# A running sum on VectorE for stick-breaking attention, and another order of its last units

## The chip, the cores and the metric

The kernel runs on one core of a Trainium2 chip. The metric is the device time of one execution in microseconds (us). TensorE (PE) multiplies matrices into PSUM, VectorE (DVE), ScalarE (ACT) and GpSimd (POOL) compute elementwise, SyncE (SP) issues the transfers. TensorE's clock is granted at one of two levels, 1.2 or 2.4 GHz; a profile gives the granted clock of a stretch as a share of the full one.

## The reference, cut to what matters

The program is two blocks of two layers each. The change is in the first block, whose layers mix four groups of heads, gate them and project them:

```python
def stick_breaking_attention(q, k, v):
    ...
    def step(args):
        qblk, i = args
        z = jnp.einsum('bqhd,bkhd->bhqk', qblk.astype(jnp.float32), kf) * scale
        qpos = i * BLOCK + jnp.arange(BLOCK)
        mask = kpos[None, :] < qpos[:, None]
        log_keep = jnp.where(mask, jax.nn.log_sigmoid(-z), 0.0)
        after = lax.cumsum(log_keep, axis=3, reverse=True) - log_keep
        a = jnp.where(mask, jnp.exp(jax.nn.log_sigmoid(z) + after), 0.0)
        return jnp.einsum('bhqk,bkhd->bqhd', a, vf)
...
    y = jnp.stack([ya, yb, yc, yd], axis=2)
    y = rmsnorm(y, g_grp.reshape(N_GROUPS, GROUP_WIDTH)).reshape(b, s, D_MIX)
    y = y * jax.nn.silu(gate)
    return x + rmsnorm(y @ w_out, g_post)
```

There are 512 positions, 4 heads of 64 in this group, and blocks of 128 keys. For each query the weight of a key needs the sum of log_keep over all later keys up to the query.

## The kernel before, in words

Everything is stored transposed, features on the partitions and the 512 positions along the free dimension, in chunks of 128 features. Matrix products with weights use fp32 split in a high and a low part (fp32r): ScalarE writes the high part of a weight slot of 128x1024 (`w_high`), GpSimd and VectorE the two halves of its low part (`w_low`), and TensorE makes three products of it, 8 matmuls each. Slots stream through a ring of four. The same is done to activations: `y_high(c)` (ScalarE, L1426) writes XH, `y_low` (VectorE for odd chunks, GpSimd for even ones, L2337) writes XL.

The order of work on each engine is written out by hand; semaphores connect them. Stick-breaking attention is cut into eight units: two pairs of heads (hp 0 and 1), and in each the key blocks k = 3, 2, 1, 0, the last first. Unit u has scores for queries from block k on, of width 512-128k for each of the two heads, in two PSUM banks (`z_banks`). Its steps are:

- `z_scores(u)`, TensorE L743 and L745: scores of both heads and the mask. From unit 2 on it waits for the exponential of unit u-2, which frees the banks.
- ScalarE L1437 to L1439: Abs, Exp and Ln into `prob_t`; then VectorE L1906 writes softplus(z) into `sp_ts`, which keeps the four blocks of the pair of heads.
- `keep_sums(u)`, TensorE L764: the scores once more, and onto them the negated sums: the block of k itself through a triangular matrix (`ntri`), each later block k2 through an all-ones matrix (`nones`), as plain fp32 matmuls. For k=0 these are four matmuls for each head, 512, 384, 256 and 128 wide.
- ScalarE L1450: the exponential of that is the weight `a_t`. After four units `stick_values(hp)`, TensorE L775, multiplies the values, and VectorE copies them (`stick_copy`, L1895).

Between the units stand pieces of other work. TensorE's loop (L830 to L848) runs for u = 1 to 8: a half product of the input projection while there are any (up to u = 5), `high_pair` of the output projection (L820, L821: y's high halves with the first two output slots, 28 and 29; two chunks at u = 7, two at u = 8), `z_scores(u)`, sums for group norms (L555), `keep_sums(u-1)`. `high_pair` at u = 7 waits for y's high halves, for the accumulators 28 and 29 (that is, for VectorE's `take` of gate chunk 7, L1753) and for both parts of the second slot. ScalarE's loop (L1428) runs the functions of unit u, the exponential of unit u-1, and the rest: slots, squares, `gate_sigmoids` (which load the sigmoid's table and load the old one back, L1418 and L1419), `y_high`. VectorE's loop (L1898) takes the last gate chunks before units 2, 4 and 6, makes low halves of slots, writes the softplus, computes a row of the second block's modulation (`modulation`, L1730, whose rows SyncE loads one by one in line with the weight slots), norms and gates.

## Time and profile before

| | us |
|---|---|
| median of the runs | 2401.52 |
| lowest and highest of 3 | 2398.0, 2401.79 |
| the profiled execution | 2396.37 |
| its span in the profile | 2394.6 |
| TensorE busy | 2254.8 (94%) |
| VectorE busy | 1655.5 (69%) |
| ScalarE busy | 1016.3 (42%) |
| mean granted clock of TensorE | 0.989 |

The span runs from the first to the last instruction; the execution's own time is 1.8 us longer. The stick-breaking units of layer 0 lie from about 221 to 307 us of the span, those of layer 1 from about 584 to 659 us for the part from the second unit on. Then each layer's output projection follows, and after layer 1 the second block, which the change does not touch. In the timelines a matmul's start is exact and its end modelled; the pitch from one start to the next is the time that it takes.

### The profile page before, as it was taken

The page shows a single profiled execution, that of the slowest core. Times are in us where ns is not written, and L with a number is a line of the kernel's source. Part 1 is how long each engine was busy: PE and PEld are TensorE (multiplying, and loading weights), DVE is VectorE, ACT ScalarE, POOL GpSimd, SP SyncE. Part 2 cuts the span into 40 slices and gives each one's busy share as a digit, 9 for nine tenths or more (in the row PEclk, how much of TensorE's full clock was granted, in tenths as well). Part 3 has the DMA queues.
Part 4 walks back from the last instruction along what each step waited for, and adds up shares of the span by engine and source line. Part 5 has one row for each costly group of instructions (what it writes and reads, how often), then busy time and mean ns, then how long its engine had stood idle before and what let it go on. Part 6 is the DMA issues. An engine that isn't in the chain of part 4 may idle for free.

```text
span 2394.6 us, 34614 instructions
## 1 busy us (share of the span) xinstructions
PE 2254.8 (94%) x11722; PEld 1774.6 (74%) x11722; DVE 1655.5 (69%) x2744; ACT 1016.3 (42%) x1665; POOL 695.2 (29%) x418
## 2 busy tenths in 40 slices
PE   8999899999788799989999999999999999999998
PEld 5766566766467689976767788888768677888886
DVE  8776578775588767545688576666566875766765
ACT  4344624344534456534254444442242634444421
POOL 3211143211142256642101333334321013333342
PEclk9999999999999999989999999999999999999999
DMA  6421234422143145543210244446531102434463
GB/s 216 168 80 54 88 106 146 158 71 71 62 158 118 52 141 184 177 143 121 78 36 1 97 141 146 144 144 225 180 133 53 37 18 88 156 134 155 140 233 140
DMA packets 81102, 286.88 MB, mean 120 GB/s; under 512 B 9009, under 2 KB 11218, under 8 KB 80564
## 3 DMA queue, kind: packets, MB, share of 16 engines
q1 hardware_dynamic: 80948, 284.95, 34.9%
q8 instruction: 81, 1.33, 0.2%
q14 instruction: 73, 0.60, 0.1%
HBM read 282.82 MB, written 2.10 MB: 119 GB/s over the span
## 4 chain that ended last, share of the span: by engine, by line
PE 49%; DVE 3%; issue 1%; ACT 1%; DVEq 0%; ACTq 0%
PE banks L1198 6%; PE banks L1204 6%; PE banks L1202 6%; PE banks L1220 3%; PE banks L1221 3%; PE banks L1227 3%; PE banks L887 3%; PE banks L888 3%; PE banks L892 3%; PE banks L1046 2%; PE banks L1065 2%; PE banks L1076 2%; PE banks L909 1%; PE banks L916 0%; DVE y_t L2216 0%
## 5 line engine op out<-in xcount | busy, mean ns | idle before, releaser
L1527 ACT ACTIVATE wh_t<-ring 128x1024 fp32r<-128x1024 f32 x264 | 279.1, 1058 | 496.6 <-PE banks L1204 297.9
L2007 DVE TENSOR_TENSOR wl_t<-ring,wh_t 128x512 fp32r<-128x512 f32 x264 | 203.3, 771 | 284.6 <-ACT wh_t L1527 279.6
L2364 POOL TENSOR_TENSOR wl_t<-ring,wh_t 128x512 fp32r<-128x512 f32 x132 | 223.1, 1693 | 470.8 <-ACT wh_t L1527 449.3
L2396 POOL TENSOR_TENSOR wl_t<-ring,wh_t 128x512 fp32r<-128x512 f32 x132 | 236.2, 1790 | 420.2 <-ACT wh_t L1527 420.1
L2331 POOL TENSOR_TENSOR wl_t<-ring,wh_t 128x512 fp32r<-128x512 f32 x72 | 126.0, 1753 | 450.6 <-ACT wh_t L1285 433.9
L1198 PE MATMUL banks<-xh_t,wh_t 128*128 128x512 f32 (+1 forms) x960 | 203.0, 354 | 0.0
L1202 PE MATMUL banks<-xh_t,wl_t 128*128 128x512 f32 (+1 forms) x960 | 203.0, 354 | 0.0
L1204 PE MATMUL banks<-xl_t,wh_t 128*128 128x512 f32 (+1 forms) x960 | 203.0, 354 | 0.0
L1220 PE MATMUL banks<-gh_t,wh_t 128*128 128x512 f32 (+1 forms) x528 | 180.5, 354 | 1.0 <-ACT wh_t L1527 1.0
L1221 PE MATMUL banks<-gl_t,wh_t 128*128 128x512 f32 (+1 forms) x528 | 180.3, 354 | 0.0
L1202 PEld LDWEIGHTS banks<-xh_t,wl_t 128*128 128x128 f32 x960 | 161.4, 189 | 25.0
L1198 PEld LDWEIGHTS banks<-xh_t,wh_t 128*128 128x128 f32 x960 | 161.4, 189 | 25.0
L1204 PEld LDWEIGHTS banks<-xl_t,wh_t 128*128 128x128 f32 x960 | 161.4, 189 | 24.9
L887 PE MATMUL banks<-xh_t,wh_t 128*128 128x512 f32 (+1 forms) x480 | 173.6, 374 | 4.1 <-ACT wh_t L1527 4.1
L888 PE MATMUL banks<-xl_t,wh_t 128*128 128x512 f32 (+1 forms) x480 | 164.0, 354 | 0.0
L1730 DVE CUSTOM_DVE_ANT_0 banks<-m_t 128x1024 f32<-128x1024 f32 x96 | 159.0, 1656 | 2.6 <-DMA m_t<-wmod_d 0.9
L2259 DVE CUSTOM_DVE_ANT_0 m_t<-m_t 128x1024 f32<-128x1024 f32 x96 | 153.1, 1595 | 5.7 <-DMA m_t<-wmod_d 4.5
L564 PE MATMUL banks<-xh_t,wh_t 128*128 128x512 f32 x320 | 127.8, 399 | 5.9 <-DVE y_t L1945 5.0
L565 PE MATMUL banks<-xl_t,wh_t 128*128 128x512 f32 x320 | 124.6, 390 | 0.0
L1227 PE MATMUL banks<-gh_t,wl_t 128*128 128x512 f32 (+1 forms) x528 | 114.6, 354 | 0.2 <-POOL wl_t L2364 0.2
L1220 PEld LDWEIGHTS banks<-gh_t,wh_t 128*128 128x128 f32 x528 | 99.8, 189 | 15.1 <-ACT wh_t L1527 1.2
L1221 PEld LDWEIGHTS banks<-gl_t,wh_t 128*128 128x128 f32 x528 | 99.8, 189 | 13.7
(394 smaller groups left out, 4562.5 us busy)
## 6 DMA issues: line engine op xcount, KB each, us to landing
ring<-w_d SPq DMA_DIRECT2D x338, 512.0 KB, 3.7
m_t<-wmod_d SPq DMA_DIRECT2D x160, 512.0 KB, 3.5
qh_t<-tables_d SPq DMA_DIRECT2D x6, 512.0 KB, 4.7
m_t<-tables_d SPq DMA_DIRECT2D x6, 512.0 KB, 5.4
par<-p_d SPq DMA_DIRECT2D x4, 696.0 KB, 6.4
x_t<-x_in_d SPq DMA_DIRECT2D x4, 512.0 KB, 6.6
big<-tables_d SPq DMA_DIRECT2D x2, 1024.0 KB
out_d<-x_t SPq DMA_DIRECT2D x4, 512.0 KB, 2.8
```

Source lines behind the costliest of these rows:

```text
L887: pe.matmul(dst, hi[:, k * P:(k + 1) * P], xh[k], start=k == 0, stop=False)
L888: pe.matmul(dst, hi[:, k * P:(k + 1) * P], xl[k], start=False, stop=False)
L1198: pe.matmul(dst, hi[:, k * P:(k + 1) * P], xh[k], start=k == 0, stop=False)
L1202: pe.matmul(dst, lo[:, k * P:(k + 1) * P], xh[k], start=False, stop=False)
L1204: mm = pe.matmul(dst, hi[:, k * P:(k + 1) * P], xl[k], start=False, stop=k == KD - 1)
L1220: pe.matmul(dst, hi[:, o:o + P], v["GH"][k + u], start=k + u == 0, stop=False)
L1221: pe.matmul(dst, hi[:, o:o + P], v["GL"][k + u], start=False, stop=False)
L1227: mm = pe.matmul(dst, lo[:, o:o + P], v["GH"][k + u], start=False, stop=k + u == FK - 1)
L1527: nc.scalar.activation(WH[j % 2], slot2(j), ACT.Copy).then_inc(sm2["w2_hi"], 1)
L2007: nc.vector.tensor_tensor(WL[j % 2][:, 512:1024], slot2(j)[:, 512:1024], WH[j % 2][:, 512:1024].bitcast(F32), ALU.subtract).then_inc(sm2[" ...
L2364: pool.tensor_tensor(WL[j % 2][:, 0:512], slot2(j)[:, 0:512], WH[j % 2][:, 0:512].bitcast(F32), ALU.subtract).then_inc(sm2["w2_lo_a"], 1)
L2396: pool.tensor_tensor(WL[q % 2][:, 0:512], slot2(24 + q)[:, 0:512], WH[q % 2][:, 0:512].bitcast(F32), ALU.subtract).then_inc(sm2["w2_lo_a"], 1)
```

## The change

Three things change.

1. VectorE adds up later blocks. When the softplus of a unit with k = 1 or 0 is written, VectorE waits until `keep_sums` of the unit before is through (`wz_ready`), and adds block k+2 onto block k+1 of `sp_ts` (all but its first 128 columns, which k+2 doesn't reach). `keep_sums` then needs one matmul through `nones` for each head, of block k+1, in place of one for each later block. It waits for the new semaphore `sp_summed`. 12 matmuls a layer go, four VectorE instructions come.
2. TensorE issues `z_scores(u)` directly behind the half product, so at u = 7 before `high_pair`.
3. ScalarE's last three gate sigmoids move from the end of step 5 into step 7, behind that unit's functions; the four high halves of y that stood in steps 6 and 7 all stand in step 6. VectorE's take of gate chunk 7 and the low half of slot 29 move behind the softplus of unit 6.

```diff
--- before.py
+++ after.py
@@ -85,7 +85,7 @@
     acc_ready=36, acc0_free=18, acc1_free=18, lat_up=8, kr_ready=1, lat_squared=3, lat_summed=2, lat_ready=3,
     qc_in=4, kvc_in=4, swap_ready=5, rot_ready=5, kr_copied=4,
     vt_ready=6, vt_copied=6, sc_ready=32, negmax=32, p_exp=32, p_norm=32, pt_ready=32, pt_copied=32,
-    o_ready=16, o_copied=16, z_ready=8, z_ln=8, sp_done=8, wz_ready=8, a_exp=8,
+    o_ready=16, o_copied=16, z_ready=8, z_ln=8, sp_done=8, sp_summed=4, wz_ready=8, a_exp=8,
     sbo_ready=2, sbo_copied=2, conv_done=2, y_squared=8, y_summed=4, y_normed=8,
     gate_sig=8, gate_mul=8, y_ready=8, z_squared=KD, z_added=KD - 2, z_summed=1, zn_ready=KD // 2, x_updated_a=4, x_updated_b=4,
     link_act=32, link_dve=LINK_DVE1,
@@ -757,12 +757,15 @@
 
                     hp, k = U[u]
                     pe.wait_ge(*at("sp_done", u + 1))
+                    if k < NT - 2:
+                        pe.wait_ge(*at("sp_summed", 2 * hp + NT - 2 - k))
                     masked_scores(u, False)
+                    last = min(k + 1, NT - 1)
                     for e, bank in enumerate(z_banks(u)):
-                        for k2 in range(k, NT):
+                        for k2 in range(k, last + 1):
                             o = e * 1280 + OFF[k2]
                             mm = pe.matmul(bank[:, (k2 - k) * P:T - k * P], ntri if k2 == k else nones, sp_ts[hp][:, o:o + T - k2 * P],
-                                           start=False, stop=k2 == NT - 1)
+                                           start=False, stop=k2 == last)
                     mm.then_inc(sm["wz_ready"], 1)
 
                 def stick_values(hp):
@@ -830,6 +833,8 @@
                 for u in range(1, len(U) + 1):
                     if pieces:
                         piece()
+                    if u < len(U):
+                        z_scores(u)
                     if u == 7:
                         acc_begin(28)
                         acc_begin(29)
@@ -839,8 +844,6 @@
                         high_pair(range(2))
                     elif u == 8:
                         high_pair(range(2, 4))
-                    if u < len(U):
-                        z_scores(u)
                     if u in (2, 3, 4):
                         group_sum(u - 2)
                     if u == 5:
@@ -1442,6 +1445,8 @@
                         w_high(26)
                     if u >= 1:
                         hp, k = U[u - 1]
+                        if u == 7:
+                            gate_sigmoids(range(5, KD))
                         act.wait_ge(*at("wz_ready", u))
                         if u == 1:
                             act.wait_ge(*at("conv_done", 2))
@@ -1456,14 +1461,10 @@
                         group_rstd(u - 2)
                     if u == 2:
                         gate_sigmoids(range(5))
-                    elif u == 5:
-                        gate_sigmoids(range(5, KD))
                     elif u == 6:
-                        y_high(0)
-                        y_high(1)
+                        for c in range(4):
+                            y_high(c)
                     elif u == 7:
-                        y_high(2)
-                        y_high(3)
                         group_square(3, (0,))
 
                 y_high(4)
@@ -1896,7 +1897,7 @@
 
                 U = units()
                 for u in range(len(U)):
-                    if u in (2, 4, 6):
+                    if u in (2, 4):
                         j = 24 + u // 2
                         take(j, H[GATE + j - 20])
                         w_low(j + 2)
@@ -1905,10 +1906,16 @@
                     dve.wait_ge(*at("z_ln", u + 1))
                     nc.vector.scalar_tensor_tensor(both(sp_ts[hp], k), z_both(u, w), 0.0, lz_both(u, w),
                                                    ALU.max, ALU.add).then_inc(sm["sp_done"], 1)
+                    if k < NT - 2:
+                        dve.wait_ge(*at("wz_ready", u))
+                        later = both(sp_ts[hp], k + 1)[:, :, P:]
+                        nc.vector.tensor_tensor(later, later, both(sp_ts[hp], k + 2), ALU.add).then_inc(sm["sp_summed"], 1)
                     if u == 0:
                         outs(TN // 2 - 1)
                         w_low(26)
                     elif u == 6:
+                        take(27, H[GATE + 7])
+                        w_low(29)
                         stick_copy(0)
                     modulation(16 + u)
                     if u in (3, 4, 5):
```

ScalarE (ACT), steps 5 to 7 of the loop, before; L1285 is a slot's high part, L1437 to L1439 the functions of a unit, L1450 an exponential, L1418 and L1419 the gate sigmoids with their tables, L1426 high halves of y:

```order
L1450 ACTIVATE big<-banks 128x2x128
L1285 ACTIVATE wh_t<-ring 128x1024
L1418 ACT_TABLE_LOAD
L1418 ACTIVATE vm_t<-big 128x512
L1418 ACTIVATE kh_t<-big 128x512 x2
L1419 ACT_TABLE_LOAD
L1437 ACTIVATE prob_t<-banks 128x2x384
L1438 ACTIVATE prob_t<-prob_t 128x2x384
L1439 ACTIVATE prob_t<-prob_t,eps_t 128x2x384
L1450 ACTIVATE big<-banks 128x2x256
L1426 ACTIVATE xh_t<-y_t 128x512 x2
L1437 ACTIVATE prob_t<-banks 128x1024
```

and now (L1440 to L1442 are the functions, L1455 the exponential, L1421 and L1422 the sigmoids, L1429 the high halves):

```order
L1288 ACTIVATE wh_t<-ring 128x1024
L1440 ACTIVATE prob_t<-banks 128x2x384
L1441 ACTIVATE prob_t<-prob_t 128x2x384
L1442 ACTIVATE prob_t<-prob_t,eps_t 128x2x384
L1455 ACTIVATE big<-banks 128x2x256
L1429 ACTIVATE xh_t<-y_t 128x512 x4
L1440 ACTIVATE prob_t<-banks 128x1024
L1441 ACTIVATE prob_t<-prob_t 128x1024
L1442 ACTIVATE prob_t<-prob_t,eps_t 128x1024
L1421 ACT_TABLE_LOAD
L1421 ACTIVATE vm_t<-big 128x512
L1421 ACTIVATE kh_t<-big 128x512 x2
```

The two table loads and three sigmoids moved from ahead of unit 6's functions to behind unit 7's, and the four high halves stand together ahead of unit 7's functions.

VectorE (DVE) around unit 6, before; L1879 and L1885 are a gate's products, L1753 the take of gate chunk 7, L1720 the low half of slot 29, L1906 the softplus, L1895 the copy of the first pair of heads, L1730 a modulation row:

```order
L1879 TENSOR_TENSOR big<-big,va_t 128x512
L1885 TENSOR_TENSOR y_t<-y_t,big 128x512
L1753 COPY big<-banks 128x512
L1720 TENSOR_TENSOR wl_t<-ring,wh_t 128x512
L1906 SCALAR_TENSOR_TENSOR big<-banks,prob_t 128x2x384
L1895 COPY y_t<-banks 128x512
L1730 ISA big,mtmp<-m_t 128x1024
```

and now (L1880, L1886, L1754, L1721, L1907, L1896 and L1731 are those; L1912 is the new sum):

```order
L1880 TENSOR_TENSOR big<-big,va_t 128x512
L1886 TENSOR_TENSOR y_t<-y_t,big 128x512
L1907 SCALAR_TENSOR_TENSOR big<-banks,prob_t 128x2x384
L1912 TENSOR_TENSOR big<-big 128x2x128
L1754 COPY big<-banks 128x512
L1721 TENSOR_TENSOR wl_t<-ring,wh_t 128x512
L1896 COPY y_t<-banks 128x512
L1731 ISA big,mtmp<-m_t 128x1024
```

The softplus and a sum of 2x128 stand ahead of the take and the slot's low half. The other three sums follow the softplus of units 2, 3 and 7 in the same way.

TensorE (PE) from unit 5's accumulation on, before; L743 and L745 are scores and mask, L764 the accumulation, L547 and L837 waits, L820 and L821 the output products (each of the last two rows comes four times in turn and stands here once):

```order
L764 MATMUL banks<-big,cst 128x128
L547 REGISTER_ALU
L837 REGISTER_ALU
L820 MATMUL banks<-xh_t,wh_t 128x512
L821 MATMUL banks<-xh_t,wl_t 128x512
L743 MATMUL banks<-big 128x512 x2
L745 MATMUL banks<-mask_r,ident_r 128x128 x2
L743 MATMUL banks<-big 128x384 x2
L745 MATMUL banks<-mask_r,ident_r 128x128 x2
L764 MATMUL banks<-big,cst 128x384
L764 MATMUL banks<-big,cst 128x256
L764 MATMUL banks<-big,cst 128x128
```

and now (L767 is the accumulation, L842 a wait, L823 and L824 the output products, the rows that only repeat left out in the same way):

```order
L767 MATMUL banks<-big,cst 128x128
L743 MATMUL banks<-big 128x512 x2
L745 MATMUL banks<-mask_r,ident_r 128x128 x2
L547 REGISTER_ALU
L842 REGISTER_ALU
L823 MATMUL banks<-xh_t,wh_t 128x512
L824 MATMUL banks<-xh_t,wl_t 128x512
L743 MATMUL banks<-big 128x384 x2
L745 MATMUL banks<-mask_r,ident_r 128x128 x2
L767 MATMUL banks<-big,cst 128x384
L767 MATMUL banks<-big,cst 128x256
```

Unit 7's scores, 512 wide, moved ahead of the output products, and unit 6's accumulation has lost the matmul 128 wide of each head.

## Rows read from the trace of the kernel before

**Rows 1.** Page, part 1: busy us (share of the span) and instructions of each engine

```profile
PE 2254.8 (94%) x11722; PEld 1774.6 (74%) x11722; DVE 1655.5 (69%) x2744; ACT 1016.3 (42%) x1665; POOL 695.2 (29%) x418
```

**Rows 2.** Waits of TensorE over the span: us in total, times, longest us

```profile
PE banks L820 <- ACT xh_t L1426: 21.2, 6, 7.6
...
PE banks L564 <- DVE y_t L1945: 5.0, 4, 2.0
```

**Rows 3.** Timeline of TensorE, layer 0: start us, us, engine, line, operation [idle before]

```profile
258.80 1.98 PE L555 MATMUL banks<-mw,cst 128*128 128x512 f32 x4 [1.48 <-ACT rstd_t L1277]
...
262.05 4.53 PE L764 MATMUL banks<-sp_even,cst 128*128 128x512 f32 x16
266.33 1.18 PE L681 MATMUL banks<-xl_t,wh_t 128*128 128x512 f32 x4
...
274.41 0.92 PE L743 MATMUL banks<-big 64*128 64x384 f32 x4 [0.47 <-ACT big L1450]
...
276.54 1.52 PE L764 MATMUL banks<-big,cst 128*128 128x256 f32 x8
285.69 0.76 PE L820 MATMUL banks<-xh_t,wh_t 128*128 128x512 f32 x1 [7.63 <-ACT xh_t L1426]
...
289.03 1.13 PE L743 MATMUL banks<-big 64*128 64x512 f32 x4
...
290.46 0.92 PE L743 MATMUL banks<-big 64*128 64x384 f32 x4
...
291.58 2.81 PE L764 MATMUL banks<-big,cst 128*128 128x384 f32 x12
295.81 0.51 PE L820 MATMUL banks<-xh_t,wh_t 128*128 128x512 f32 x1 [1.42 <-ACT xh_t L1426]
...
299.20 4.53 PE L764 MATMUL banks<-big,cst 128*128 128x512 f32 x16
304.93 2.38 PE L775 MATMUL banks<-big,vd_t 128*64 128x512 f32 x16 [1.19 <-ACT big L1450]
```

**Rows 4.** Busy us by stretch: PE, PEld, DVE, ACT, POOL, then PEclk, DMA share, GB/s

```profile
285.70:289.00 3.30, 3.30 (x8) 2.39 (x8) 3.27 (x5) 0.36 (x1) 1.19 (x1) 0.56 0.05 11
...
320.40:355.70 35.30, 34.83 (x148) 27.73 (x149) 34.56 (x41) 7.92 (x11) 21.31 (x12) 1.00 0.51 179
```

**Rows 5.** Timeline of ScalarE (ACT), layer 0, around the gate sigmoids

```profile
275.32 1.28 ACT L1418 ACT_TABLE_LOAD   x1
...
279.95 0.63 ACT L1418 ACTIVATE kh_t<-big 128x512 f32<-128x512 f32 x1 [2.19 <-DVE big L1753]
...
281.89 0.81 ACT L1437 ACTIVATE prob_t<-banks 128x768 f32<-128x768 f32 x1
...
284.45 0.58 ACT L1450 ACTIVATE big<-banks 128x512 f32<-128x512 f32 x1
284.93 1.14 ACT L1426 ACTIVATE xh_t<-y_t 128x512 fp32r<-128x512 f32 x2
290.57 1.02 ACT L1437 ACTIVATE prob_t<-banks 128x1024 f32<-128x1024 f32 x1 [4.50 <-PE banks L745]
```

**Rows 6.** Timeline of VectorE (DVE), layer 0

```profile
255.52 1.23 DVE L1906 SCALAR_TENSOR_TENSOR sp_even<-banks,prob_t 128x1024 f32<-128x1024 f32 x1 [10.88 <-ACT prob_t L1439]
...
275.50 1.76 DVE L1879 TENSOR_TENSOR big<-big 128x512 f32<-128x512 f32 x1
...
279.23 0.68 DVE L1753 COPY big<-banks 128x512 f32<-128x512 f32 x1
279.83 0.68 DVE L1720 TENSOR_TENSOR wl_t<-ring,wh_t 128x512 fp32r<-128x512 f32 x1
284.57 0.96 DVE L1906 SCALAR_TENSOR_TENSOR big<-banks,prob_t 128x768 f32<-128x768 f32 x1 [4.06 <-ACT prob_t L1439]
...
293.89 1.23 DVE L1906 SCALAR_TENSOR_TENSOR big<-banks,prob_t 128x1024 f32<-128x1024 f32 x1 [4.58 <-ACT prob_t L1439]
```

**Rows 7.** Timeline of GpSimd (POOL), layer 0

```profile
275.38 1.33 POOL L2331 TENSOR_TENSOR wl_t<-ring,wh_t 128x512 fp32r<-128x512 f32 x1 [16.38 <-ACT wh_t L1285]
```

## The prediction

> **What bounds the kernel now.** I read the page's busy shares first: TensorE is busy 94% of the span [rows 1], so only work taken off TensorE, or a wait in front of it, can pay. The list of waits then shows where it idles: its longest wait in total is L820, the first output products, for ScalarE's high halves of y (L1426), 21.2 us in six waits, the longest 7.6 [rows 2]. Each layer runs the stretch once, so a layer has half of that. TensorE's timeline of layer 0 shows the place [rows 3]: the cumulative matmuls (L764) of unit 5 start at 276.54, and after them TensorE stands still 7.63 us until 285.69; another 1.42 us end at 295.81. I read the rest of the argument from the stretch 262 to 305 of layer 0; layer 1 has the same waits (21.2 is twice 10.6) and is taken as equal.
>
> Why it waits is in ScalarE's timeline [rows 5]: at 275.32 it loads another function table, computes three sigmoids (the last held 2.19 us by VectorE's take of gate chunk 7), loads the old table back, and only at 281.89 begins unit 6; y's first two high halves come at 284.93. The granted clock was 0.56 in the 3.3 us behind the wait, so TensorE had fallen from 2.4 to 1.2 GHz while it stood still, and the eight products there took 3.34 us (285.69 to 289.03) [rows 3, 4].
>
> **The change, part by part.** All times in layer 0.
>
> *Fewer matmuls.* L764 of a unit with k=0 took 4.28 us (262.05 to 266.33) for 5120 record columns (4 records for each width: two heads, two records per fp32 matmul), 0.836 ns each [rows 3]. The change keeps widths 512 and 384: 3584 columns, 3.00 us, so 1.28 less. A unit with k=1 keeps 384 and 256 of 384, 256, 128: 0.43 less. Units with k=2 and 3 keep everything. That is 1.71 for each pair of heads, 6.8 us over two pairs and two layers. Of it the 0.43 of unit 2 is worth nothing: behind it TensorE waits 1.48 us for ScalarE anyway (258.80), and the wait grows by 0.43 [rows 3]. Unit 3's 1.28 is on the path, and everything behind it starts 1.28 earlier.
>
> *The running sum.* Four more VectorE instructions a layer, 2x128 wide for k=1 and 2x256 for k=0. No row shows this operation. The nearest is VectorE's subtraction of two SBUF operands 512 wide: 0.68 alone, 1.76 when GpSimd was in such a subtraction (its own began at 275.38 and took 1.33) [rows 6, 7]. So 0.3 to 1.76 for one; less than nothing is excluded, it is added work. I take 0.7 for k=0 and, where GpSimd works beside it, 0.9. Each sum also waits until the unit before has been accumulated, since that read the block unsummed; queued behind it stand the modulation row, gates, and so SyncE's next modulation load. Nothing is charged for units 2 and 3: before unit 3's softplus at 255.52 VectorE stood idle for 10.88 us, which takes up what unit 2's sum adds, and TensorE comes to unit 3's accumulation at 262.05, some 5 us after a sum that follows that softplus [rows 3, 6]. Unit 7: the previous accumulation ends at 286.9 (below), the sum is ready about 288.0, and TensorE is in the second pair of output chunks until 288.9: hidden by 0.9, with 1.76 it is just not.
>
> *The new order.* In my reckoning, TensorE ends unit 5's accumulation at 276.54+1.28-1.28 = 276.54. Unit 6's scores began at 274.41, now 273.1, ready about 274.4 [rows 3]. ScalarE is free at 275.32-1.28 = 274.0 because the sigmoids are gone from here; unit 6's three functions take 2.56 (281.89 to 284.45) and end at 277.0, its exponential of unit 5 at 277.6 [rows 5]. TensorE waits for that, 1.1 us, then runs unit 7's scores, which now come first: 1.43 (289.03 to 290.46), until 279.1 [rows 3]. ScalarE makes four high halves in a row, 0.57 each, from 277.6 to 279.8 [rows 5].
>
> Now VectorE is late next. Gate 3's product ended at 279.23, now 278.0 [rows 6]. Then come unit 6's softplus 0.96, the sum 0.9, the take of chunk 7 at 0.6 (279.23 to 279.83; it frees the accumulator that the output products need) and the low half of slot 29, between 0.68 and 1.76, taken at 1.2, since GpSimd is making low halves of y at that time. That is 281.65, when the output products start instead of 285.69: a wait of 2.55. The waits 7.63 and 1.42 are replaced by 1.1 and 2.55.
>
> The rest at full clock: first output pair 2.0 (3.39 from 295.81 to 299.20, less the 1.4 of scores in it), scores 1.12 (290.46 to 291.58), accumulation 2.56-0.43 = 2.13, ending at 286.9 [rows 3]. Unit 7's functions: ScalarE from 279.8, 3.3 us (290.57 to VectorE's start at 293.89), then the two tables and three sigmoids, which took 6.57 (275.32 to 281.89) less the 2.19 of wait, 4.4; all done at 287.5, then unit 6's exponential [rows 5, 6]. No one waits for that one. Second output pair with scores 3.39, without a wait as its halves are long made: 290.3. Accumulation 3.00: 293.3. Wait for the last exponential as before, 304.93-299.20-4.28 = 1.45 [rows 3]: the value matmuls L775 start at 294.75 instead of 304.93. **10.2 us a layer, 20.4 in both.** From L775 on the order is the same on every engine, and the 35.3 us behind it (320.40 to 355.70) have TensorE busy 34.83 of it [rows 4], so the gain passes on.
>
> The profiled execution took 2396.37 us, which gives 2376.0. The median of the runs shown stands 5.15 above it, at 2401.52, and 20.4 off that gives 2381.1. I predict 2381.
>
> **A rule weighed.** VectorE's gate product that began at 275.50 ended 0.55 us after GpSimd's 1.33 us were over [rows 6, 7]. The Trainium skill, page "SBUF — State Buffer", section "Who interferes with whom", says that a VectorE instruction with two SBUF inputs and a GpSimd one that reads SBUF exclude each other for their whole length, whoever starts first. By that rule the sum waits for GpSimd's first low half and slot 29's subtraction for its second: output products at about 281.6 and 20.4 us in all; if they ran undisturbed, 280.6 and 22.5 us. The trace agrees with the rule, and it speaks against a sum placed where four high halves set GpSimd to work.
>
> **Bounds of the forecast.** Undisturbed, VectorE is done at 280.6: 11.2 a layer, 2379. If both two-operand instructions take 1.76, it is 283.0: 8.9 a layer. If the clock also falls in the waits of 1.1 and 2.55 (one of 2.0 at L564 left it at 1.00 [rows 2, 4], the long one didn't), 1.4 a layer is lost (3.34 against 2.0 for a pair): 7.5 a layer, 2386.5. The runs shown spread 3.8 us.
>
> **Rivals.**
> 1. *The sum is on the path.* If unit 6's and unit 7's sums and their two hand-overs each hold TensorE for one contended subtraction, 1.76, a layer gains 10.2-3.5 = 6.7: 2388. For it: unit 7 has 0.9 us to spare. Against: units 2 and 3 have far more, and ScalarE's sigmoids are off this path.
> 2. *The long wait only changes its owner.* The output products need chunk 7's take and slot 29, both now behind the softplus of unit 6; if that is reached as late as the present 284.57 [rows 6], the products start near 287 and only the trimmed matmuls and the second wait remain: about 3.4 a layer at most, 2395. Against: 284.57 is caused by the sigmoids, which are gone.
> 3. *The stretch behind is fed too slowly.* It starts 10 us earlier, and in it the transfers use 0.51 of the DMA engines, at 179 GB/s [rows 4]. If two slots are late by 2 us each in each layer: 2389. Against: those slots are asked for by events that move along.
> 4. *The change does not save what it says*, as when the compiled order kept the sigmoids in front of the halves; the order shows that it doesn't. Nothing moves: 2401.
> 5. *Slower.* After the two waits TensorE stays at 1.2 GHz. From 281.65 to 294.75 it has 11.7 us of work, which would take 23.4; that alone costs 11.7 a layer against a gain of 10.2. The mechanism decides from 10.2 us of work at the low clock a layer on; at the full 11.7, it is 3 us slower, 2404.5, and more where it lasts into the output projection. For it: TensorE now idles twice within 5 us with only 1.43 of work between. Against: behind a wait of 7.63 the low clock lasted about 3.3 us.
>
> **How the numbers follow.** Forecast 0.76 (2379 to 2386.5), rival 1 0.09, rival 3 0.05, rival 2 0.04, rival 4 0.03, slower 0.03. A measurement of this kernel can tell about 0.2%, 4.8 us, from no change. Faster by more than that: the forecast and rivals 1 and 3 wholly, and 2 nearly, 0.94; same 0.03 (rival 4); slower 0.03. The range goes from 2375 (the upper bound of the gain, less the spread of the runs) to 2388.5 (rival 1 included).
>
> **What would show it.** L767 of a k=0 unit at 3.0 us; the wait before L823 near 2.5 instead of 7.6, ended by VectorE's slot subtraction and no longer by the high halves; granted clock 1.00 throughout 276 to 290; L778's second group near 294.7; no wait that VectorE's sum ends. Wrong: a wait of TensorE on the sum over 1 us, a clock of 0.6 after 281, or new DMA waits in the output projection.

## The result, and the profile after

| | before | after |
|---|---|---|
| median, us | 2399.76 (4 runs, 2396.89 to 2401.79) | 2381.72 (4 runs, 2380.27 to 2384.13) |
| the profiled execution, its span | 2396.37, 2394.6 | 2380.27, 2378.4 |
| TensorE busy | 2254.8 | 2249.5 |
| mean granted clock of TensorE | 0.989 | 0.989 |

The change is faster: the ratio is 0.9925, with a 95% interval of 0.9911 to 0.9939, so 18.0 us by the medians and between 14.6 and 21.4. The forecast was a gain of 20.4 and a time of 2381. The time was met within a microsecond, but part of that is luck: the gain inside the two stretches that the change touches was 15.1 us in the profiled pair, and two clock falls in each layer, which the sum had left out, make the difference. Laid from profile to profile, the forecast was 2376.0 and the measured time 2380.27.

The page of the changed kernel, part 1, as [rows 1]:

```profile
PE 2249.5 (95%) x11674; PEld 1767.7 (74%) x11674; DVE 1656.3 (70%) x2752; ACT 1015.3 (43%) x1665; POOL 687.5 (29%) x418
```

48 records of TensorE are gone (12 fp32 matmuls a layer, two records each, in two layers), and 8 instructions of VectorE have come. TensorE's waits, as [rows 2]: us in total, times, longest.

```profile
PE banks L823 <- DVE wl_t L1721: 4.7, 2, 2.4
...
PE banks L555 <- ACT rstd_t L1280: 3.4, 2, 1.7
PE banks L823 <- ACT xh_t L1429: 3.1, 2, 1.6
PE banks L743 <- ACT big L1455: 3.0, 6, 0.9
```

The waits of 7.63 and 1.42 for the high halves of y are gone. In their place stand 2.4 for VectorE's low half of slot 29 and 0.9 for ScalarE ahead of unit 7's scores. (What is left of L823 for `xh_t` are two waits of 1.56 in the output projection; before has them too.) No wait is ended by VectorE's sum. TensorE's timeline of layer 0, to be read against [rows 3]:

```profile
259.87 3.52 PE L555 MATMUL banks<-mw,cst 128*128 128x512 f32 x4 [1.70 <-ACT rstd_t L1280]
263.32 1.13 PE L743 MATMUL banks<-big 64*128 64x512 f32 x4
...
264.65 3.22 PE L767 MATMUL banks<-sp_even,cst 128*128 128x512 f32 x8
267.42 1.38 PE L681 MATMUL banks<-xl_t,wh_t 128*128 128x512 f32 x4
268.64 2.00 PE L685 MATMUL banks<-xh_t,wl_t 128*128 128x512 f32 x8
...
280.21 1.13 PE L743 MATMUL banks<-big 64*128 64x512 f32 x4 [0.87 <-ACT big L1455]
...
284.09 0.76 PE L823 MATMUL banks<-xh_t,wh_t 128*128 128x512 f32 x1 [2.38 <-DVE wl_t L1721]
287.39 0.92 PE L743 MATMUL banks<-big 64*128 64x384 f32 x4
...
293.98 3.22 PE L767 MATMUL banks<-big,cst 128*128 128x512 f32 x8
298.39 2.37 PE L778 MATMUL banks<-big,vd_t 128*64 128x512 f32 x16 [1.19 <-ACT big L1455]
```

Two things are to be seen. The third group sum (L555) took 3.52 us instead of 1.98, behind a wait that had grown from 1.48 to 1.70. And the first pair of output products took 3.30 (284.09 to 287.39), where 2.0 had been reckoned. Both are the clock, in the same four matmuls and the same eight. Busy us by stretch, PEclk the third from the end:

```profile
259.90:263.30 3.40, 3.40 (x4) 1.14 (x4) 3.40 (x7) 1.78 (x4) 0.00 (x0) 0.54 0.38 134
...
284.10:287.40 3.30, 3.30 (x9) 2.35 (x9) 3.27 (x6) 3.24 (x5) 0.00 (x0) 0.58 0.57 184
```

The group sum of before had PEclk 1.00. In layer 1 of the change both fell too (the group sum took 3.68, the pair 3.44).

VectorE, as [rows 6]: the four sums (L1912), and what stands between unit 6's softplus and the output products.

```profile
245.05 0.43 DVE L1912 TENSOR_TENSOR sp_even<-sp_even 128x256 f32<-128x256 f32 x1 [0.49 <-PE banks L767]
...
257.74 0.68 DVE L1912 TENSOR_TENSOR sp_even<-sp_even 128x512 f32<-128x512 f32 x1
...
280.53 0.95 DVE L1907 SCALAR_TENSOR_TENSOR big<-banks,prob_t 128x768 f32<-128x768 f32 x1
281.40 0.92 DVE L1912 TENSOR_TENSOR big<-big 128x256 f32<-128x256 f32 x1
282.24 0.68 DVE L1754 COPY big<-banks 128x512 f32<-128x512 f32 x1
282.84 1.15 DVE L1721 TENSOR_TENSOR wl_t<-ring,wh_t 128x512 fp32r<-128x512 f32 x1
...
290.92 0.69 DVE L1912 TENSOR_TENSOR big<-big 128x512 f32<-128x512 f32 x1 [2.73 <-PE banks L767]
```

and GpSimd beside it, as [rows 7]:

```profile
280.76 2.68 POOL L2344 TENSOR_TENSOR xl_t<-y_t,xh_t 128x512 fp32r<-128x512 f32 x2 [2.75 <-ACT xh_t L1429]
```

The sum 256 wide took 0.43 alone and 0.92 while GpSimd made low halves of y; the slot's low half took 1.15 instead of 0.68. ScalarE, as [rows 5]: unit 7's functions, both table loads behind them, and then still 1.22 us of idle time before unit 6's exponential. The sigmoids are off the path.

```profile
282.14 1.01 ACT L1440 ACTIVATE prob_t<-banks 128x1024 f32<-128x1024 f32 x1
...
285.44 1.28 ACT L1421 ACT_TABLE_LOAD   x1
...
288.42 1.28 ACT L1422 ACT_TABLE_LOAD   x1
290.92 0.82 ACT L1455 ACTIVATE big<-banks 128x768 f32<-128x768 f32 x1 [1.22 <-PE banks L767]
```

**How the experiments are read.** The executions of one program spread by up to 14 us, much of it outside the changed code, so each run is also read by the *stretch*: from the start of the layer's first group sum (L555) to the start of the second value matmuls (L775 or L778), which holds all that the change moves on TensorE from unit 2 on. Before it is 65.28 us in layer 0 (239.65 to 304.93) and 65.48 in layer 1. The change has 57.67 and 57.97: 7.6 and 7.5 less. "Group sum" and "pair" below are the time from the first matmul of the third L555 group, or of the first output products, to the next scores: 1.91 and 2.0 at full clock. Where the low clock lasts longer than the group or the pair, the scores behind it are slow too, and the table does not show that part; it is named below where it matters.

| run | stretch, layers 0 and 1 | wait, group sum (0; 1) | wait, pair (0; 1) |
|---|---|---|---|
| before | 65.28, 65.48 | 1.48, 1.91; 1.48, 1.92 | 7.63, 3.34; 7.63, 3.56 |
| the change | 57.67, 57.97 | 1.70, 3.45; 1.70, 3.61 | 2.38, 3.30; 2.37, 3.44 |
| after_again | 59.16, 56.41 | 1.70, 3.40; 1.70, 1.92 | 2.38, 3.68; 2.38, 3.16 |
| sum_only | 63.00, 64.44 | 1.70, 1.92; 1.70, 3.01 | 7.63, 3.68; 7.63, 3.68 |
| order_only | 56.60, 58.23 | 1.48, 1.92; 1.48, 2.81 | 1.06, 2.02; 1.06, 2.01 |
| take_first | 55.12, 55.03 | 1.70, 3.33; 1.70, 3.56 | 0.97, 2.02; 0.97, 1.99 |
| scores_behind | 57.61, 58.21 | 1.70, 1.91; 1.70, 3.56 | 3.33, 3.68; 3.33, 2.87 |
| sigmoids_back | 62.09, 62.16 | 1.70, 3.55; 1.70, 3.34 | none, 2.84; none, 2.94 (7.02 ahead of the scores) |
| order_take | 56.47, 56.51 | 1.48, 1.91; 1.48, 1.92 | 0.97, 1.99; 0.97, 2.02 |
| order_take_again | 58.04, 56.45 | 1.48, 1.91; 1.48, 1.91 | 0.97, 3.36; 0.97, 1.99 |
| change_fill7 | 56.47, 54.89 | 1.70, 3.55; 1.70, 1.92 | 0.17, 2.00; 0.18, 2.02 |
| change_filled | 54.84, 54.86 | 0.35, 1.91; 0.35, 1.91 | 0.17, 2.00; 0.18, 2.02 |
| fill_wait | 53.38, 53.39 | 0.35, 1.91; 0.35, 1.91 | 0.97, 1.99; 0.97, 1.99 |
| fill_again | 54.86, 53.42 | 0.35, 1.92; 0.35, 1.91 | 0.97, 3.47; 0.96, 2.01 |

### The profile page after: what moved, and what is told of

Same layout as the page of the kernel before. It is cut to its first block, busy times and chain, and to the rows that moved or that the text cites. A ratio compares the mean times of both kernels' runs of the same rounds, so it can differ in the third digit from the quotient of the medians.

```text
span 2378.4 us, 34534 instructions
## 1 busy us (share of the span) xinstructions
PE 2249.5 (95%) x11674; PEld 1767.7 (74%) x11674; DVE 1656.3 (70%) x2752; ACT 1015.3 (43%) x1665; POOL 687.5 (29%) x418
## 3 DMA queue, kind: packets, MB, share of 16 engines
q8 instruction: 80, 1.31, 0.2%
## 4 chain that ended last, share of the span: by engine, by line
PE 50%; DVE 3%; issue 1%; ACT 1%; DVEq 0%; ACTq 0%
PE banks L1207 6%; PE banks L1205 6%; PE banks L1201 6%; PE banks L1224 3%; PE banks L1230 3%; PE banks L1223 3%; PE banks L890 3%; PE banks L891 3%; PE banks L895 3%; PE banks L1049 2%; PE banks L1079 2%; PE banks L1068 2%; PE banks L912 1%; PE banks L907 1%; PE banks L908 1%
## 5 line engine op out<-in xcount | busy, mean ns | idle before, releaser
L2014 DVE TENSOR_TENSOR wl_t<-ring,wh_t 128x512 fp32r<-128x512 f32 x264 | 203.2, 771 | 286.4 <-ACT wh_t L1528 281.8
L2371 POOL TENSOR_TENSOR wl_t<-ring,wh_t 128x512 fp32r<-128x512 f32 x132 | 223.0, 1692 | 466.5 <-ACT wh_t L1528 445.0
L2403 POOL TENSOR_TENSOR wl_t<-ring,wh_t 128x512 fp32r<-128x512 f32 x132 | 236.3, 1791 | 420.1 <-ACT wh_t L1528 420.0
L2338 POOL TENSOR_TENSOR wl_t<-ring,wh_t 128x512 fp32r<-128x512 f32 x72 | 119.0, 1655 | 459.9 <-ACT wh_t L1288 443.9
L1731 DVE CUSTOM_DVE_ANT_0 banks<-m_t 128x1024 f32<-128x1024 f32 x96 | 156.8, 1633 | 3.1 <-DMA m_t<-wmod_d 1.4
L564 PE MATMUL banks<-xh_t,wh_t 128*128 128x512 f32 x320 | 129.5, 405 | 5.0 <-DVE y_t L1952 4.1
L1721 DVE TENSOR_TENSOR wl_t<-ring,wh_t 128x512 fp32r<-128x512 f32 x72 | 62.6, 870 | 69.0 <-ACT wh_t L1288 67.8
```

Source lines behind the costliest of these rows:

```text
L2014: nc.vector.tensor_tensor(WL[j % 2][:, 512:1024], slot2(j)[:, 512:1024], WH[j % 2][:, 512:1024].bitcast(F32), ALU.subtract).then_inc(sm2[" ...
L2371: pool.tensor_tensor(WL[j % 2][:, 0:512], slot2(j)[:, 0:512], WH[j % 2][:, 0:512].bitcast(F32), ALU.subtract).then_inc(sm2["w2_lo_a"], 1)
L2403: pool.tensor_tensor(WL[q % 2][:, 0:512], slot2(24 + q)[:, 0:512], WH[q % 2][:, 0:512].bitcast(F32), ALU.subtract).then_inc(sm2["w2_lo_a"], 1)
```

## The experiments

### The change taken apart

**The change once more** (no edit).

> The changed kernel once more, beside the others on one chip. If the lower clock behind the wait of 1.7 us at L555 (the four sums took 3.5 us and not 2.0 there) is the change's own, it shows again in both layers; if it was chance, at most one layer shows it. Time against the kernel before: 16 to 20 us less.

Measured: 2382.81 us (2381.15 to 2386.15, 5 runs), ratio 0.993 (0.9917 to 0.9944). The change's time holds. In layer 1 the group sum kept its clock behind the same wait of 1.70, so that fall does not come every time. The pair fell in both layers; in layer 1 its first two matmuls were still quick (0.47 and 0.39) and the rest slow, 3.16 for the eight. In layer 0 the low clock lasted beyond the pair: the scores behind it took 1.58 for 0.85 from start to start, and the fall cost 2.8 us in all, 1.5 more than in the first profile.

**Only the running sum**, on the order of before.

```
+ (VectorE, behind the softplus of units with k < 2)
+     nc.vector.tensor_tensor(later, later, both(sp_ts[hp], k + 2), ALU.add)
- for k2 in range(k, NT):
+ for k2 in range(k, min(k + 1, NT - 1) + 1):
```

> The running sum and the fewer matmuls alone, the order of the kernel before. Theory 1 (my terms stand, the clock at L555 was chance): 1.28 of unit 3, 0.43 of unit 6 (hidden in the wait of 1.42, so nothing) and 1.28 of unit 7 a layer, 2.6 to 3.0 a layer, 5.1 to 6.0 us in all. Theory 2 (fewer matmuls in unit 2 make the wait in front of the sums L555 longer, 1.70 for 1.48, and the clock falls there): the same less 1.5 a layer, so only 2 to 3 us, and L555 at 3.5 us. The wait of 7.6 us in front of the first output product stays under both.

Measured: 2396.82 us (2392.53 to 2399.89, 11 runs), ratio 0.9986 (0.9977 to 0.9995), so some 3 us; the stretches are 2.3 and 1.0 shorter. With what the clock took counted back (in layer 0 0.8 more than in before, behind the wait of 7.63; in layer 1 0.4 there and 1.65 in the group sum and the scores behind it) the sum is worth 3.1 in either layer. The waits of 7.63 and 1.42 stand as they were. The wait before the group sum grew here too, and in layer 1 the clock fell behind it:

```profile
609.68 3.08 PE L555 MATMUL banks<-mw,cst 128*128 128x512 f32 x4 [1.70 <-ACT rstd_t L1280]
```

So the longer wait comes with the running sum and the trimmed matmuls of unit 2, not with the new order.

**Only the new order**, with all matmuls and without the sum.

```
- (VectorE) the sum, its semaphore and TensorE's wait for it
- for k2 in range(k, last + 1):
+ for k2 in range(k, NT):
```

> The new order alone, with all the matmuls and no sum. Theory 1: 7.2 a layer as in my sum, and 0.9 more because VectorE has no sum ahead of the low half of slot 29: 16 us in all; the wait in front of the first output product about 1.5. Theory 2 adds: the sums L555 take 2.0 us again behind a wait of 1.48, and the time is no more than 2 us above the whole change's. If the clock falls before the output products in this one too, it is 1.3 a layer less: 13.6 us.

Measured: 2382.18 us (2379.69 to 2387.63, 5 runs), ratio 0.9933 (0.9919 to 0.9946). On the same chip the whole change took 2382.81. The order alone gives the whole gain, and on top of it the sum adds nothing that the medians show. TensorE in layer 0:

```profile
282.17 0.47 PE L820 MATMUL banks<-xh_t,wh_t 128*128 128x512 f32 x1 [1.06 <-DVE wl_t L1718]
...
296.96 2.38 PE L775 MATMUL banks<-big,vd_t 128*64 128x512 f32 x16 [1.19 <-ACT big L1452]
```

This stretch began 0.71 later than before's (240.36 against 239.65), so the output products start at 281.46 on the clock of before. In the change they start at 284.09, less 1.07 of later begin and 1.54 of fallen clock in the group sum (3.45 for 1.91 to the next scores): 281.5. The same moment. What the sum takes off TensorE ahead of the products is waited away before them (1.06 has become 2.38), since VectorE is what they wait for and the sum costs it as much: 0.84 of its own (281.40 to 282.24), and the slot's low half behind it took 1.15 where it takes 0.68 here. Only the matmuls behind the products can pay. With the clock held they do: 56.60 here in layer 0, with no fall, against 54.84 in the change with its waits filled (below), 1.8 for the reckoned 0.43+1.28. In the change as it is the two clock falls took that back.

### VectorE's order

**Take first.** The whole change, but VectorE takes chunk 7 and makes slot 29's low half ahead of unit 6's softplus, as before.

```
-                    if u in (2, 4):
+                    if u in (2, 4, 6):
...
-                        take(27, H[GATE + 7])
-                        w_low(29)
```

> The whole change, but VectorE takes gate chunk 7 and makes the low half of slot 29 before unit 6's softplus and its sum, as the kernel before did. If the wait of 2.38 us in front of the output products is VectorE's order alone, it shrinks to about 0.5 and the clock does not fall: 1.9 and 1.3 a layer, 6.4 us less than the changed kernel. Rival: GpSimd's two low halves of y hold slot 29's subtraction wherever it stands, so that it ends no earlier than 283 and at most 1 us a layer is won.

Measured: 2375.5 us (2374.33 to 2376.59, 4 runs), ratio 0.99 (0.9885 to 0.9915): 7 us faster than the change on the same chip. The wait before the output products shrank to 0.97, and behind it the pair ran at full clock in both layers. VectorE's row of the low half, which now ends before the softplus starts:

```profile
281.34 1.46 DVE L1721 TENSOR_TENSOR wl_t<-ring,wh_t 128x512 fp32r<-128x512 f32 x1
282.72 0.94 DVE L1907 SCALAR_TENSOR_TENSOR big<-banks,prob_t 128x768 f32<-128x768 f32 x1
```

The stretch is 2.6 and 2.9 shorter than the change's: 1.5 from the earlier products (54.85 against 53.39 between the two filled kernels), the rest from the clock of the pair. The group sum fell in both layers still.

**The same without the running sum.**

> take_first without the sum and with all the matmuls: what the running sum is worth once nothing waits for it. By the terms: 1.28 in unit 3, 0.43 in unit 6, 1.28 in unit 7, so 3.0 a layer and 6 us more than take_first. Theory 2 (a longer wait in unit 4 costs the clock more often): 1 to 1.5 us of that is lost again, 4.5 to 5 us.

Measured: 2386.76 us median of 6 runs, from 2375.92 (the profiled one) to 2389.62, ratio 0.9946 (0.9932 to 0.996). The stretches, 56.47 and 56.51, are the order's without a clock fall; against 53.39 in the filled kernel with the sum they put the sum's worth at 3.1 us a layer, once nothing takes it back. But the median is over 10 us above the profiled execution. The mean granted clock on record goes with it: 0.992 in the profiled one, 0.987 to 0.989 in the five others (2385.29 to 2389.62). Where in the span they lost it no trace shows. So it was run again, below.

### The two other parts of the order

Both on take_first. **The last gate sigmoids back in ScalarE's step 5:**

```
-                        if u == 7:
-                            gate_sigmoids(range(5, KD))
...
+                    elif u == 5:
+                        gate_sigmoids(range(5, KD))
```

> take_first with the last three gate sigmoids back in ScalarE's step 5. If their place is the core of the gain: TensorE waits about 7 us for unit 5's exponential ahead of unit 7's scores, 5.4 a layer more than in take_first, and the clock falls there (1.3 more): 13 us more, near 2389. Rival: the gain came from TensorE's order, and this costs less than 4 us.

Measured: 2387.47 us (2385.93 to 2393.42, 6 runs), ratio 0.9948 (0.9934 to 0.9963). TensorE waits in front of unit 7's scores, and starts them at the low clock:

```profile
287.85 2.08 PE L743 MATMUL banks<-big 64*128 64x512 f32 x4 [7.02 <-ACT big L1453]
```

The stretches are 7.0 and 7.1 longer than take_first's. In layer 0 5.2 of that is waiting (7.02, where take_first has 0.87 ahead of the scores and 0.97 ahead of the products), and 1.9 is the clock: from start to start the scores took 2.01 for 1.06, the mask behind them 0.49 for 0.37, and the pair 2.84 for 2.0. Of the parts taken back one by one, the sigmoids' place is worth the most.

**Unit 7's scores behind the first output products again:**

```
-                    if u < len(U):
-                        z_scores(u)
                     if u == 7:
...
                     elif u == 8:
                         high_pair(range(2, 4))
+                    if u < len(U):
+                        z_scores(u)
```

> take_first with unit 7's scores behind the first output products again. The scores' 1.43 us no longer fill the wait, so one wait of 3.5 us stands in front of the products: 1.4 a layer, 2.9 us more than take_first; with the clock falling in it 2.7 a layer, 5.5 us more. Rival: nothing, if ScalarE's chain sets the end of unit 7 anyway.

Measured: 2381.75 us (2376.25 to 2385.05, 5 runs), ratio 0.9917 (0.9901 to 0.9934). The wait before the output products is 3.33, and the clock fell behind it in both layers:

```profile
281.64 0.77 PE L823 MATMUL banks<-xh_t,wh_t 128*128 128x512 f32 x1 [3.33 <-DVE wl_t L1721]
```

The stretches are 2.5 and 3.2 longer than take_first's. The scores are work that fills the wait: 1.4 is their own time (289.03 to 290.46 in [rows 3]), and the pair behind it lost 1.7 and 0.9 to the clock. The low clock lasted into the scores behind the pair, which took 1.99 and 1.78 from start to start in place of 1.06, another 0.9 and 0.7:

```profile
285.32 2.05 PE L743 MATMUL banks<-big 64*128 64x512 f32 x4
```

In layer 0 the group sum kept its clock, where take_first's fall had cost 1.65 (1.4 in the sum, 0.2 in the scores behind it). That adds up to 2.4 and 3.0 of the 2.5 and 3.2.

### The price of the clock, by filling the waits

**take_first with the group sum's wait filled.** TensorE multiplies into a free bank while it would stand still; nobody reads the result.

```
+                    if u == 4:
+                        pe.wait_ge(*at("o_copied", TN // 2))
+                        for _ in range(3):
+                            pe.matmul(ps[7][:, 0:256], ident, cst[:, 0:256], start=True, stop=True)
```

> The kernel with VectorE's take first, and three matmuls of no use (256 wide, fp32, into a bank that is free there) in TensorE's wait in front of the third group sum L555. Clock theory: TensorE no longer falls to 1.2 GHz in that wait of 1.70 us, the four sums take 2.0 us in both layers in place of 3.4 to 3.6, so about 1.5 a layer and up to 3 us less than take_first. Rival: the sums were slow for another reason (a memory conflict with ScalarE and VectorE), and the time stays within 1 us.

Measured: 2373.72 us (2371.72 to 2374.26, 4 runs), ratio 0.9888 (0.9873 to 0.9904). The group sum kept its clock in both layers, and the stretches are 1.7 and 1.6 shorter than take_first's.

**The change itself, both waits filled**, the second with five such matmuls into accumulator 28, which the first product then overwrites.

```
                         acc_begin(28)
+                        for _ in range(5):
+                            pe.matmul(accs[0][:, 0:256], ident, cst[:, 0:256], start=True, stop=True)
                         acc_begin(29)
```

> The changed kernel with both of its new waits filled by matmuls whose result nobody reads: three of 128x256 into a free bank ahead of the third group sum (the wait of 1.70 us), five of 128x256 into output accumulator 28 before its first real product (the wait of 2.38 us, for VectorE's low half of slot 29). Theory, that the missing part of the forecast gain is the clock that falls in these two waits, priced at 1.5 for the four group-sum matmuls and 1.3 for the first pair of output products in each layer: group sum 1.98 in both layers, the pair 2.0 instead of 3.3, together up to 5.6 us less, 2376 to 2378. Rival, that the price lies in the waits themselves or is given back later: 2381 to 2383, as the change.

Measured: 2377.59 us (2374.69 to 2378.45, 5 runs), ratio 0.9898 (0.988 to 0.9915). Layer 0; L852 and L841 are the fillings:

```profile
258.47 1.51 PE L852 MATMUL banks<-cst 128*128 128x256 f32 x6
260.33 1.98 PE L555 MATMUL banks<-mw,cst 128*128 128x512 f32 x4 [0.35 <-ACT rstd_t L1286]
...
280.48 2.37 PE L841 MATMUL banks<-cst 128*128 128x256 f32 x10
283.03 0.47 PE L823 MATMUL banks<-xh_t,wh_t 128*128 128x512 f32 x1 [0.17 <-issue]
285.03 0.92 PE L743 MATMUL banks<-big 64*128 64x384 f32 x4
...
296.01 2.37 PE L778 MATMUL banks<-big,vd_t 128*64 128x512 f32 x16 [1.19 <-ACT big L1461]
```

This is the forecast's own case, the change at full clock, and its numbers can be laid beside the forecast. The stretch began 1.52 later than before's, so the output products start at 281.51 on the clock of before (forecast 281.65) and L778 at 294.49 (forecast 294.75). The stretches are 10.4 and 10.6 shorter than before's, where 10.2 had been reckoned. All matmuls of the change are in it, and eight more, and still it is 2.8 to 3.1 us a layer shorter than the change.

**Only the second wait filled.**

> The changed kernel with only the later wait filled, by five matmuls of 128x256 ahead of the first output products. Clock theory: pair of output products 2.0 in both layers, group sum still slow behind its wait of 1.70 in most executions: 2379 to 2380. If the fills delay the products, since they still run when the low half is ready: 2382 or more.

Measured: 2381.03 us (2377.75 to 2381.45, 6 runs), ratio 0.9912 (0.9896 to 0.9928). The pair took 2.00 in both layers; the group sum fell in layer 0 and not in layer 1, and the two stretches differ by just that, 56.47 and 54.89.

**The best version again.**

> The best version once more (the take of gate chunk 7 and the low half of slot 29 ahead of unit 6's softplus, three matmuls in the wait before the third group sum): 2372 to 2375 in every execution if the two clock falls are what varied between executions; a spread over 5 us speaks for another cause.

Measured: 2377.19 us (2372.33 to 2379.14, 6 runs), ratio 0.9896 (0.9878 to 0.9914). The spread of 6.8 us is over what had been expected, so the two falls are not all that varies. In this profile the pair of layer 0 fell behind a wait of 0.97 that had left it alone in fill_wait.

**order_take again.**

> The new order with the early take and without the running sum, all matmuls kept, once more. Its first study had one execution, the profiled one, at 2375.9 and five at 2385 to 2390. If the clock in the group sum (wait of 1.48) and in other short waits decides, the executions fall again into two levels, and a profile of a long one shows L555 at 3.4 in one or both layers; by the sum of parts it is 2375.5 plus 6.8 less 3 to 6 of clock, 2377 to 2380 at full clock. Rival, that 2376 was a single odd execution and the cause is elsewhere: all near 2387.

Measured: 2384.56 us (2379.96 to 2388.91, 6 runs), ratio 0.9929 (0.991 to 0.9948). The executions did not fall into two levels, and the expectation of slow group sums was wrong: both were at full clock. The fall came in the pair of layer 0, within the second matmul:

```profile
281.54 0.47 PE L820 MATMUL banks<-xh_t,wh_t 128*128 128x512 f32 x1 [0.97 <-issue]
281.85 0.56 PE L821 MATMUL banks<-xh_t,wl_t 128*128 128x512 f32 x1
282.20 0.63 PE L820 MATMUL banks<-xh_t,wh_t 128*128 128x512 f32 x1
```

The larger part lies elsewhere: from the last value matmuls of layer 1 to the end of the span this execution took 1740.9 us, that of order_take 1734.5, on the same instructions.

## Why the prediction was right, and where it was wrong

- **What bounds the kernel**: right. With the rest in place, taking the sigmoids from ahead of unit 6 is worth 7.0 us a layer (sigmoids_back), and the order alone has the whole gain (order_only).
- **Fewer matmuls**: right in size. From L767's start to L685's it was 3.99 us (264.65 to 268.64) in place of 5.30 (262.05 to 267.35), so 1.31 for the reckoned 1.28.
- **"Of it the 0.43 of unit 2 is worth nothing"**: this step failed. It took the longer wait for free. Unit 2's trimmed matmuls made the wait before the group sum 1.70 instead of 1.48 (the rest of the 0.43 went into a new wait of 0.16 before the scores ahead of it), and behind 1.70 the clock fell in 10 of 14 profiled layers, behind 1.48 in 1 of 8. A fall cost 1.5 and 1.7 us in the change, about four times what was saved, and as much in every other profile that has one (1.5 to 1.7, with the slow scores behind the sum counted). sum_only has it with the old order, and in the filled kernels (wait 0.35) it came in none of 6 layers. Those kernels have the trimmed unit 2 and the wait of 0.16 ahead as well, so it is the idle time in the longer wait that matters; whether the 0.16 adds to it is not separated.
- **VectorE late next**: right, to 0.15 us. The wait for slot 29's low half was 2.38 (forecast 2.55), VectorE's instructions ahead of it took 0.95, 0.92, 0.60 (this one from start to start) and 1.15 (forecast 0.96, 0.9, 0.6 and 1.2), and the products started at 281.5 on the clock of before (forecast 281.65).
- **"The rest at full clock: first output pair 2.0"**: the second step that failed; it had been named as a bound. The pair took 3.30 and 3.44, and filling the wait brings 2.00 back. The prediction's own sign of being wrong, a clock of 0.6 after 281, came true: 0.58 from 284.10 to 287.40, where it had asked for 1.00 throughout 276 to 290. Its doubt had rested on the wait of 2.0 at L564 that left the clock alone; one such wait says little, since the same wait can be followed by a fall in one layer and by none in the next.
- **The sum of the terms**: 10.2 a layer was 10.4 and 10.6 with the clock held (change_filled), and 7.6 and 7.5 without. The bound "if the clock also falls in the waits" had 7.5 a layer, 15 us, and the stretches of the profiled pair gave 15.1. That agreement is luck: the bound is made of one clock fall at 1.4 and of 1.3 for VectorE's two instructions at 1.76 each, which took 0.92 and 1.15; what filled its place was a second fall, in the group sum, which it did not have. The span fell by 16.2: the stretches 15.1 less, the parts ahead of and between them 1.9 more (1.07 and 0.83), the part behind them 3.0 less, with the same instructions. So the forecast gain was 2.4 over the 18.0 of the medians, and the time was met because the median of before, 2401.52 in the runs shown, came down by 1.8 to 2399.76 with one more. The medians in turn gained more than the stretches, and the granted clock on record says much of why: in 15 further executions of before on one chip, the six at 0.989 took 2397.1 to 2398.3, the nine at 0.985 to 0.987 took 2398.9 to 2404.3. The four executions of the change at 0.989 (three here, one of after_again) took 2380.3 to 2382.2. At equal clock, then, the gain is about 16, near the 15.1 and 16.2 of the profiled pair, and not 20.
- **Rival 1, the sum on the path**: not as put; no wait of TensorE ends with it. But it costs in another way, through VectorE's queue, where slot 29's low half stands behind it. That queue, not TensorE's, times the output products, and it is why the trimmed matmuls ahead of them brought nothing.
- **Rival 2**: no; the products did not wait for a late unit 6. **Rival 3**: no; it wanted 4 us a layer behind the stretches. From layer 0's stretch to layer 1's it was 286.65 for 285.82 (285.81 in after_again), and behind the second stretch 1735.4 for 1738.4. **Rival 4**: no. **Rival 5**: the clock fell, but for one group each time in this profile, and in its longest case (layer 0 of after_again) it lasted through the pair and into unit 6's scores and accumulation, never to the end of the stretch.
- **The rule weighed** (the Trainium skill, page "SBUF — State Buffer", section "Who interferes with whom"): the sum 256 wide took 0.43 with GpSimd idle and 0.92 with GpSimd at work, the low half 1.15 or 1.46 for 0.68. The trace agrees with the rule in that both were held. In order_only it was GpSimd that was held: its two low halves of y took 3.06 in place of 2.68, with slot 29's subtraction, at 0.68, in the middle of them. So who comes first decides who pays, and the sum changed that too. It was right to place its price in VectorE's queue ahead of the output products: they started at 281.5, where the forecast had about 281.6 with it and 280.6 without.

**The better version.** take_first with the filled wait had ratios of 0.9888 (0.9873 to 0.9904) and 0.9896 (0.9878 to 0.9914), where the change had 0.9925 and 0.993: some 8 us more, 4.4 a layer by the stretches (57.8 against 53.4, where the pair keeps its clock). Of the 4.4, 3.0 are the clock (the change against the change filled, 54.85) and 1.5 VectorE's order (54.85 against 53.4). Over take_first itself (0.99, 0.9885 to 0.9915) the intervals show no gain; there only the stretches show what the filling is worth.

**What stays open.** Why order_take's medians (2386.76, 2384.56) lie above order_only's 2382.18, with stretches that are no longer. In part it is the clock: order_only's executions had 0.990 or 0.991 but for one, order_take's in both runs 0.987 to 0.990 but for one. Where they lost it is not shown. And how often each of the later clock falls comes: the part behind the second stretch, untouched by every kernel here, took from 1734.5 to 1742.4 us in 14 profiles (1738.4 before, 1735.4 after). One place shows it. Both rows are of the change, from the same stretch of the second block, in the first profile and in after_again:

```profile
800.00:820.00 20.00, 13.88 (x103) 12.52 (x104) 15.24 (x28) 6.33 (x15) 5.25 (x6) 1.00 0.00 1
```

```profile
800.00:820.00 20.00, 14.77 (x86) 13.11 (x87) 12.85 (x26) 5.04 (x13) 3.19 (x5) 0.83 0.00 1
```

PEclk was 1.00 in the one and 0.83 in the other. Between 803 and 812 us the second execution fell behind the first by another 2.0 us (0.2 later at the one matmul, 2.25 at the other).

## What to carry to other kernels

Work taken from ahead of a wait is not free even where the wait absorbs it: a wait a few tenths of a microsecond longer can drop TensorE's clock, and the matmuls behind it then cost more than was saved. So price every short wait that a change makes or lengthens with what the next group costs at the low clock (here 3.45 for 1.91, 3.30 for 2.0), and try to fill it, with real work (here the next unit's scores) or, as a test, with matmuls that nobody reads. And where the bound passes from one engine to the next, what counts is the queue of the engine that is late next: here two VectorE instructions ahead of unit 6's softplus instead of behind it were worth 7 us by the medians (5.5 in the stretches, the clock of the pair included), and the 24 matmuls that the running sum saved added nothing that the medians show to the order alone, though they are worth 3.1 us a layer where nothing takes it back.

## What the runs showed of the hardware that I had not expected

- The same program loses its clock behind the same wait in one layer or execution and not in the next. By the length of the wait: 0.35 (filled), group sum slow in 0 of 6 profiled layers; 1.48, in 1 of 8; 1.70, in 10 of 14. For the first output pair: 0.17 (filled), 0 of 4; about 1.0, 2 of 12; 2.38, 4 of 4; 3.33, 2 of 2; 7.63, 4 of 4. These are counts in this kernel's surroundings; the rows say nothing of others.
- A short wait can be as dear as a long one. With what was slow behind the pair counted, a fall there cost 1.5 and 1.6 behind 0.97; 1.3, 1.4, 1.6 and 2.8 behind 2.38; 2.6 and 1.6 behind 3.33; 1.3, 1.6, 1.9 and 2.2 behind 7.63. A fall in the group sum cost 1.5 to 1.7 each time. What makes one last longer than another is not shown.
- It can begin behind the first matmul and not in it (0.47, 0.56, then 0.63 each, in order_take_again).
- The spread between executions of one program goes with the mean granted clock: on one chip before took 2397.1 to 2398.3 at 0.989 and 2401.5 to 2404.3 at 0.985 and 0.986.
